# Two-block transformer layer on one Trainium2 core: bias rows of the second expert loop copied into PSUM instead of multiplied in, and one low half in 24 made by GpSimd

## The reference, cut to what matters

```
gu   = t @ w_gu[e] + b_gu[e]          # 2048 columns: 1024 gate, 1024 up
gate = min(gu[:, :1024], 7)
up   = clip(gu[:, 1024:], -7, 7)
h    = (up + 1) * gate * sigmoid(1.702 * gate)
y   += share[e] * (h @ w_dn[e] + b_dn[e])
```

## Time and profile before

| what | value |
|---|---|
| median of three runs | 2695.45 us |
| profiled execution, first to last instruction (its span; the page gives no other time of it) | 2697.9 us |
| busy share of the span: PE, DVE, ACT, POOL | 91%, 80%, 61%, 20% |
| mean granted PE clock | 0.945 of full speed |
| second expert loop | about 1418 to 2668 us of the span |

### The profile page before, as it was taken

One profiled execution on the slowest core, in us unless ns is written; L12 is line 12 of the kernel. 1 busy time (PEld: TensorE's weight loads), 2 busy tenths in 40 slices (PEclk: granted clock), 3 DMA queues, 4 the chain that ended last, 5 costly groups with the idle time before them and its releaser, 6 DMA issues. The chain is left out here.

```text
span 2697.9 us, 38997 instructions
## 1 busy us (share of the span) xinstructions
PE 2455.0 (91%) x11864; PEld 2006.4 (74%) x11864; DVE 2165.1 (80%) x2484; ACT 1639.6 (61%) x1922; POOL 532.6 (20%) x362
## 2 busy tenths in 40 slices
PE   7987858999979998788949999999999999999994
PEld 6846646878768887677737888888888888888883
DVE  7887657999854427886468999999999999999995
ACT  3255536777744326564217777777777777777773
POOL 1213011223200003100021122222222222222220
PEclk9988868999989998999959999999999999999997
DMA  9873236999953410201238999999999999999995
GB/s 347 285 281 107 57 132 246 360 371 383 371 192 111 141 56 1 94 1 63 81 132 310 378 368 364 367 364 366 380 373 366 362 362 362 368 374 377 370 363 169
DMA packets 258910, 711.98 MB, mean 264 GB/s; under 512 B 41377, under 2 KB 74416, under 8 KB 256594
## 3 DMA queue, kind: packets, MB, share of 16 engines
q1 hardware_dynamic: 232626, 640.70, 64.0%
q0 software_dynamic: 22240, 59.81, 7.8%
q10 hardware_dynamic: 3968, 10.49, 1.0%
HBM read 691.95 MB, written 41.49 MB: 272 GB/s over the span
## 5 line engine op out<-in xcount | busy, mean ns | idle before, releaser
L51 PE MATMUL psum_all<-sb_ring_r,sb_arena_r 128*128 128x512 f32 (+1 forms) x2352 | 909.0, 386 | 0.0
L165 DVE TENSOR_TENSOR sb_ring_r<-sb_ring,sb_hi_ring_r 128x1024 fp32r<-128x1024 f32 (+1 forms) x489 | 658.7, 1397 | 124.3 <-ACT sb_hi_ring_r L156 118.5
L156 ACT ACTIVATE sb_arena_r<-sb_ring 128x1024 fp32r<-128x1024 f32 (+1 forms) x462 | 507.5, 1153 | 160.4 <-DMA sb_ring<-in_w_gu_dram 141.6
L165 DVE TENSOR_TENSOR sb_ring_r<-sb_ring,sb_arena_r 128x1024 fp32r<-128x1024 f32 (+1 forms) x462 | 594.0, 1345 | 10.8 <-ACT sb_arena_r L156 10.4
L156 ACT ACTIVATE sb_hi_ring_r<-sb_ring 128x1024 fp32r<-128x1024 f32 (+1 forms) x489 | 554.9, 1193 | 41.9 <-DMA sb_ring<-in_w_in_dram 18.2
L51 PEld LDWEIGHTS psum_all<-sb_ring_r,sb_arena_r 128*128 128x128 f32 x2352 | 447.8, 190 | 93.0
L50 PE MATMUL psum_all<-sb_hi_ring_r,sb_arena_r 128*128 128x512 f32 (+1 forms) x1304 | 497.8, 382 | 15.3 <-DVE sb_ring_r L165 5.2
L52 PE MATMUL psum_all<-sb_hi_ring_r,sb_arena_r 128*128 128x512 f32 (+1 forms) x1304 | 493.7, 379 | 0.0
L50 PE MATMUL psum_all<-sb_arena_r 128*128 128x512 f32 x1064 | 426.8, 401 | 2.5 <-DVE sb_arena_r L2424 2.5
L52 PE MATMUL psum_all<-sb_arena_r 128*128 128x512 f32 x1080 | 427.7, 396 | 0.0
L50 PEld LDWEIGHTS psum_all<-sb_hi_ring_r,sb_arena_r 128*128 128x128 f32 x1304 | 248.4, 190 | 68.5 <-issue 10.2
(11 more groups left out here) (484 smaller groups left out, 3231.8 us busy)
## 6 DMA issues: line engine op xcount, KB each, us to landing
sb_ring<-in_w_gu_dram SPq DMA_DIRECT2D x544, 512.0 KB, 6.3
sb_ring<-in_w_dn_dram SPq DMA_DIRECT2D x272, 512.0 KB, 8.5
sb_ring<-in_w_e_gate_dram SPq DMA_DIRECT2D x36, 1024.0 KB, 7.7
sb_ring<-in_w_e_up_dram SPq DMA_DIRECT2D x36, 1024.0 KB, 7.9
sb_ring<-in_w_e_down_dram SPq DMA_DIRECT2D x36, 1024.0 KB, 7.3
sb_ring<-in_w_in_dram SPq DMA_DIRECT2D x27, 1024.0 KB, 6.5
sb_arena<-in_w_ada_dram POOLq DMA_DIRECT2D x32, 512.0 KB, 5.7
sb_ring<-in_w_mod_dram SPq DMA_DIRECT2D x16, 1024.0 KB, 8.3
```

The source lines that it names most:

```text
L51: eng.matmul(out, a[0], b[1], start=False, stop=False)
L156: act.activation(s.hi[c % len(s.hi)], s.raw[c % len(s.raw)], ACT.Copy).then_inc(s.hi_made, 1)
L165: dve.tensor_tensor(s.lo[c % len(s.lo)], s.raw[c % len(s.raw)], s.hi[c % len(s.hi)].bitcast(F32), ALU.subtract).then_inc(s.lo_made, 1)
```

## The change

The bias matmuls, the selectors and the high and low halves of the bias go. In their place, for each item:

- SP loads the one row of `b_gu` that the item's expert needs (8 KB) into partition 0 or 32 of the tile `rows`, in turns (`bias_row`). Ahead of it SP waits until POOL has widened the first half of the row of the item before (`bias_wide`).
- POOL, after the gather for the next item has landed, spreads that row over all 128 partitions with two `partition_broadcast` of 1024 columns each (`widen`), each once ACT has used the old content of that half (`seeded`).
- ACT copies the wide bias into the two gate banks after the sigmoid of the item before, and into the two up banks after it has read the transposed h (`seed`, two activations of 128 x 1024 from SBUF to PSUM).
- PE's matmuls then only add to what is in the banks, and wait for `seeded`.

Also, the low half of one chunk in 24 (l = 18, the third up chunk) is made by POOL with a tensor_tensor instead of by DVE, and PE waits for it (`pool_lo`). For the first item, `route` ends with one `partition_broadcast` of 2048 columns on POOL, and DVE copies the wide bias into the banks. The core of the diff:

```diff
@@ route @@
-                sp.wait_ge(s.logits, 1)
-                for half in range(2):
-                    sp.dma_start(k.rows[32 * half:32 * half + m.experts].rearrange("p a d -> p (a d)"), b_up
-                                 ).then_inc(R.bias_landed, 16)
             sp.wait_ge(s.items, 1)
             e = sp.value_load(R.expert_i[0:1, 0:1], min_val=0, max_val=E - 1)
+            if biased:
+                sp.wait_ge(s.logits, 1)
+                for i in range(2):
+                    row = e if i == 0 else sp.value_load(R.expert_i[0:1, 1:2], min_val=0, max_val=E - 1)
+                    sp.dma_start(bias_row(k, i), b_up[bass.ds(row, 1)]).then_inc(R.row_landed[i], 16)
...
+            if biased:
+                pool.wait_ge(R.row_landed[0], 16)
+                pool.partition_broadcast(bias_wide(k), bias_row(k, 0))
+def bias_row(k, parity):
+    return k.rows[32 * parity:32 * parity + 1].rearrange("p a d -> p (a d)")
+def bias_wide(k):
+    return k.arena[:, BIAS_AT:BIAS_AT + 2 * D]
@@ experts, sync @@
+                        if biased:
+                            sp.wait_ge(s.bias_wide, 2 * j - 1)
+                            sp.dma_start(bias_row(k, (p + 1) % 2), m.bias[0][bass.ds(expert(j + 1), 1)]
+                                         ).then_inc(R.row_landed[(p + 1) % 2], 16)
@@ experts, gpsimd @@
+            def widen(half, j, parity, count):
+                pool.wait_ge(R.row_landed[parity], 16 * count)
+                pool.wait_ge(s.seeded, 2 * j - 1 + half)
+                pool.sem_inc(s.settled, 1)
+                row = bias_row(k, parity)[:, half * m.width:(half + 1) * m.width]
+                pool.partition_broadcast(seeds[half], row).then_inc(s.bias_wide, 1)
+                pool.wait_ge(s.bias_wide, 2 * j - 1 + half)
...
                         gather(j + 1)
+                        if biased:
+                            pool.wait_ge(s.gathered, 16 * j + 32)
+                            widen(0, j + 1, (p + 1) % 2, i + 2)
+                            widen(1, j + 1, (p + 1) % 2, i + 2)
+                            c = POOL_LO - nB
+                            pool.wait_ge(ss.hi_made, PER * j + c + 1)
+                            pool.tensor_tensor(ss.lo[c % len(ss.lo)], ss.raw[c % len(ss.raw)],
+                                               ss.hi[c % len(ss.hi)].bitcast(F32), ALU.subtract).then_inc(s.pool_lo, 1)
                         scatter(j - 1)
@@ experts, tensor @@
+                    if per and c == POOL_LO - nB:
+                        pe.wait_ge(s.pool_lo, j)
                     if i == 0 and biased:
-                        for b in range(BANKS):
-                            at_col = (BANKS * half + b) * 512
-                            pe.matmul(k.psum[:, UP + BANKS * half + b, :], sel_up[p], bias_hl[:, at_col:at_col + 512],
-                                      start=True, stop=False)
+                        pe.wait_ge(s.seeded, 2 * j + half + 1)
@@ experts, scalar @@
+            def seed(half, j):
+                act.wait_ge(s.bias_wide, 2 * j - 1 + half)
+                act.wait_ge(s.part_read, 2 * j - 1 + half)
+                act.activation(up_banks(half), seeds[half], ACT.Copy).then_inc(s.seeded, 1)
...
                             if l == HT_BEFORE + after(1):
                                 read_h(j - 1)
+                                seed(1, j)
                             if l == nA + after(2):
                                 sigmoid(j)
+                                seed(0, j + 1)
@@ experts, vector @@
-                            make_lo(dve, k, ss, c, PER, j, c in WHOLE)
+                            make_lo(dve, k, ss, c, PER, j, c in WHOLE or l == POOL_LO)
-                            select(sel_up[(p + 1) % 2], j + 1, s.sel_up)
```

More of the change, by code:

```diff
@@ L44, with split3 @@
 SKIP = 4096
+BIAS_AT = 22528
 CONTEXT_BANKS = (4, 5, 6, 0)
[L48 to L52, removed]
+def split3(eng, out, a, b, start, stop, seeded=False):
+    eng.matmul(out, a[0], b[0], start=start, stop=False, skip_group_check=seeded)
+    eng.matmul(out, a[0], b[1], start=False, stop=False, skip_group_check=seeded)
+    return eng.matmul(out, a[1], b[0], start=False, stop=stop, skip_group_check=seeded)
 def chain(eng, sem):
@@ L1795, in route @@
     R.bias_landed = nc.alloc_semaphore(name=f"{name}_bias_landed")
+    R.row_landed = [nc.alloc_semaphore(name=f"{name}_row_landed{i}") for i in range(2)]
     biased = m.bias is not None
@@ L2073, in experts @@
     WHOLE = m.whole
+    POOL_LO = nB + nA + 2 if m.bias is not None else PER
     HT_BEFORE = SPLIT * max(1, nA // SPLIT - 2)
@@ L2094, in experts @@
     if biased:
-        bias_hl = take(m.bias[0].shape[1], True)
-        bias_raw = k.rows[0:64].rearrange("p a d -> p (a d)")
-        sel_up = [take(P, True) for _ in range(2)]
+        seeds = [bias_wide(k)[:, half * m.width:(half + 1) * m.width] for half in range(2)]
         b_down, comb_t = k.pair.rearrange("p a d -> p (a d)"), take(P)
@@ L2101, in experts @@
     more_hi = [take(CHUNK, True) for _ in range(SLOTS - HI_SLOTS)]
-    assert at[0] <= ARENA
+    assert at[0] <= (BIAS_AT if biased else ARENA)
     FIRST = SLOTS * SPLIT
@@ L2200, in _ @@
             if biased:
+                pool.wait_ge(s.gathered, 32)
+                widen(0, 1, 1, 1)
+                widen(1, 1, 1, 1)
                 pool.wait_ge(R.y_ready, 16 * TT)
@@ L2256, in up @@
                             ins = split3(pe, out, (x_hi[p][:, kd, :], x_lo[p][:, kd, :]), [x[:, kk, cols] for x in w],
-                                         kd == 0 and not biased, kd == KD - 1)
+                                         kd == 0 and not biased, kd == KD - 1, biased)
                     ins.then_inc(ss.chunk_used, 1)
@@ L2380, in _ @@
                     sigmoid(0, False)
+                    if biased:
+                        seed(0, 1)
             with act.Fori(0, PAIRS) as i:
@@ L2407, in _ @@
             n = dve.value_load(R.last[0:1, 0:1], min_val=0, max_val=R.max_items - 1) + 1
-            def select(dst, j, sem):
-                dve.tensor_scalar(dst[0:64, :], wide(k.half_row[:, 0], 1, P), R.expert_f[0:64, bass.ds(j, 1)], None,
-                                  ALU.is_equal).then_inc(sem, 1)
             def lo_x(j, p):
@@ L2457, in _ @@
             if biased:
-                dve.memset(bias_hl[64:P, :].bitcast(F32), 0.0)
-                for sel in sel_up:
-                    ins = dve.memset(sel[64:P, :].bitcast(F32), 0.0)
-                ins.then_inc(s.bias_zero, 1)
-                dve.wait_ge(R.bias_landed, 96)
-                dve.tensor_copy(bias_hl[0:64, :], bias_raw).then_inc(s.bias_hi, 1)
-                dve.wait_ge(s.bias_hi, 1)
-                dve.tensor_tensor(bias_hl[32:64, :], bias_raw[32:64, :], bias_hl[32:64, :].bitcast(F32),
-                                  ALU.subtract).then_inc(s.bias_lo, 1)
-                select(sel_up[0], 0, s.sel_up)
-                select(sel_up[1], 1, s.sel_up)
+                for half in range(2):
+                    dve.wait_ge(s.y_made, half + 2)
+                    dve.tensor_copy(up_banks(half), seeds[half]).then_inc(s.seeded, 1)
             make_lo(dve, k, ss, 0)
```

17 lines of the change are left out of this document (7 added, 10 removed).

## The result

The changed kernel takes 2728.75 us (median of 4 runs, 2723.62 to 2745.65) against 2697.14 of the kernel before on the same chip (4 runs, 2695.42 to 2699.04): ratio 1.0127, 95% interval [1.0109, 1.0145]. It is slower by 1.3%, where 2682.6 was forecast. The profiled execution took 2731.62 us, its span is 2729.9.

What follows compares the result with a forecast made beforehand. PE sets the pace at 36.24 us an item, DVE and DMA close behind; afterwards DVE bounds at 33.20 + 2.1 + 0.55 = 35.85, over 33 items 12.9 us faster, so 2682.6 us (forecast's own range 2672 to 2692, whole range 2664 to 2744).

Steps and rivals of the forecast that it cites:

- floor 35.32: PE in the second loop: removing two pairs of bias matmuls saves 0.92 us an item, down to 35.32.
- DVE's exclusion: DVE's low halves wait while POOL reads SBUF: 2.1 us an item for POOL's low half, 0.55 for broadcasts.
- I count half of one broadcast, with its tail, as felt: 0.55: DVE: first broadcast hides beside PSUM work, second partly behind a wait for ACT; cost 0.55 us an item.
- DVE's idle time: DVE in the loop: idle 0.96 and 0.75 us an item before; expected to shrink to nearly none.
- DMA: Transfers in the loop: floor between 34.4 and 36.2 us an item, 35.3 taken, so not the bound.
- ACT's sigmoid seed and SP: Gate-bank seed covered by ACT's 1.28 us idle before the sigmoid; SP's new wait covered by some 7 us.
- Ends: Outside the loop: routing stage and start of the experts, set to 0 in sum, between -2 and +4 us.
- The sum: Item falls from 36.24 to 35.85 us, bound by DVE; over 33 items 12.9 us faster.
- The first rival: Both broadcasts stop DVE, 1.2 us each: 37.7 an item, 2743.6 us, slower; chance 0.27.
- The two signs named for the forecast being wrong: DVE not slowed at all by POOL's low half, or a broadcast taking over 2 us.
- Transfers: Rival: transfers bound the loop, an item stays at 36.1 to 36.24 us, 2691 to 2695 in all; chance 0.13.
- POOL starves: Rival: DVE holds up POOL's low half, PE waits at l = 18, over 2825 us; 0.10 together with longer broadcasts.

Runs made afterwards that it cites:

- e2: Changed kernel without the second loop's two broadcasts an item (items 1 to 33 add item 0's bias row), POOL's low half kept; 2674.3 us.
- e3: Changed kernel without both the loop's broadcasts and POOL's low half, seeds kept; 2677.09 us.
- e6: Changed kernel without POOL's low half, each broadcast of the second loop replaced by a POOL memset of the same tile; 2674.75 us.
- e4: Kernel before with only POOL's low half of l = 18 added, bias matmuls and selector kept; 2695.93 us, ratio 0.9992.
- e1: Changed kernel with DVE making all 24 low halves, none on POOL; broadcasts and seeds kept; 2719.46 us.
- e13: Changed kernel without POOL's low half, with ACT's seed of the up banks behind the high half of l = 11, not 7; 2701.12 us.
- e11: Changed kernel without POOL broadcasts or POOL's low half; each bias half written to all 128 partitions by DMA from DRAM; 2711.9 us.
- e12: Changed kernel with item 0's bias spread by a DMA in the routing stage instead of POOL's broadcast, loop untouched; 2722.73 us.
- e10: Changed kernel without POOL's low half; broadcasts beside DVE's PSUM reads, gather between them, up seed later, item 0's bias by DMA; 2669.33 us.
- e5: Changed kernel without POOL's low half, broadcasts moved beside DVE's PSUM reads, gather queued behind both; 2731.55 us.
- e9: Changed kernel without POOL's low half, broadcasts beside PSUM reads, up seed later, plus an 8-column broadcast starting the routing stage; 2723.82 us.

## Why the prediction was wrong

**PE.** Right: floor 35.32 worked out, 35.27 to 35.30 measured wherever DVE had room (e2, e3, e6).

**DVE's exclusion.** The mechanism was right, and it was priced at 2.1 for POOL's low half (measured 1.76; 1.59 in e2, 1.58 in e4) and 0.55 for the broadcasts. The second is one of the two steps that failed: "I count half of one broadcast, with its tail, as felt: 0.55". Measured are 1.16 in the changed kernel, where by luck some first broadcasts lie beside L2470, and 1.81 to 1.92 with both beside low halves (e1, e13). The 1.2 guessed for one alone was near (1.30). What was wrong was its place. The broadcast was taken to start at the gather's landing, and that to lie where DVE reads PSUM. It starts 6.6 to 9.1 us after the landing, behind the change of kind on POOL, for which the prediction had no term; and the place was checked for the old frame only, though it shifts with the item's length and POOL's other work.

**DVE's idle time.** This is the other step that failed, and the larger. The sum had none left, without a reason given. Measured is 1.00 an item: 10.7 us in the loop for the high half behind the seed of the up banks, 8.2 for PE after POOL's late low half, 6.6 for the reading of h, the rest in short gaps. The prediction covered the seed of the gate banks with the sigmoid. For the one behind L2351 it said only that the low half "must wait for ACT anyhow", and took the wait as a hiding place, not as a cost. e13 gives its price where it occurs in every item: 0.6 an item, 18 us. In the changed kernel, where it occurs in every second one, it is 0.35. The other two parts were not varied by themselves.

**DMA.** Right in kind: not the bound at 13.3 MB an item (376 GB/s in e3, PE never idle). e11 shows how close it is: with 1 MB more an item the transfers bound, at 392 GB/s.

**ACT's sigmoid seed and SP.** Covered, as said: in e3 both stand, and the floor is reached.

**Ends.** Set at 0, between -2 and +4; measured 5.5 late at the loop's start, 7.9 if counted from the first row of the routing stage on POOL (1364.8 in place of 1367.2). The broadcast's duration was right (2.30 within 1.9 to 4.7), but the 8.50 us ahead of it was no row of the trace before. e12 puts its price at some 6 us, on a wide interval.

**The sum.** 35.85 was forecast; 33.20 + 1.16 + 1.76 + 1.00 = 37.1 came. The difference is 0.61 more for the broadcasts, 0.34 less for POOL's low half and 1.00 of idle time. The forecast's gain was 0.39 an item, a difference between sums of 36. Without the idle time the item would have had about its old length (36.12); the idle time turned the sign. The first rival had the right bound (DVE past 36.24), the right sign and nearly the right price (37.7 an item forecast, 37.03 found; "2.4 of broadcasts" was too much, and no idle time was in it); 2728.75 lies inside the range. The first rival's signs came too: slowed low halves beside broadcasts, PE waiting for L166, a pitch over 36.3. The two signs named for the forecast being wrong did not (DVE was slowed by POOL's low half, and a broadcast took 1.87): they looked at durations, and what failed was a place and a wait. *Transfers* did not happen. *POOL starves* did not happen in the changed kernel as it was told, by a low half that can't get in; but its sign, PE waiting for POOL at l = 18, did, 21.5 us in all, because the low half started late. e10's one bad item shows that POOL can starve.

Open is how much of the shift from e1's 2.0 low halves an item beside broadcasts to the changed kernel's 1.29 is due to the 6.6 to 9.1 us and how much to POOL's low half shifting the scatter and so the gather (neither was varied by itself), what POOL does in that time, and what decides whether a broadcast or the low halves go first when both want to run.

Exclusion for the whole instruction, which the prediction took from the Trainium skill (SBUF — State Buffer, Who interferes with whom) as the ground of its rival, is borne out: 0.9 us for a broadcast beside low halves (e1), none beside PSUM readers (e5), none from memsets (e6). That page gives the ports to whoever issues first; in e10's bad item a copy that takes 0.75 otherwise ran for 14.54 us, while DVE started and ended ten low halves, so the turn seems not to go by time of issue alone.

## What to carry to other kernels

Where DVE is the bound and its instructions have two inputs in SBUF, work moved to POOL unloaded DVE here only where POOL's instruction did not read SBUF, or where DVE was just then reading PSUM: 1.14 us moved away cost 1.6 to 1.8, and the same two broadcasts cost low halves 1.8 to 1.9 us or, by place, 0.7 and less (e10, e5). Tie such an instruction to a count of the engine that it must not meet, not to a transfer's landing, and look at once at what is queued behind it. Look in POOL's queue for MODIFY_POOL_CONFIG before letting two kinds of instruction take turns there. And where the forecast gain is a hundredth of a sum, list the idle times of the new bound engine as terms of their own before calling a sign.

## What was not expected of the hardware

- A partition_broadcast of 1 row to 128 x 1024 takes POOL 1.30 us alone and 1.87 on average in the changed kernel's loop; beside low halves it stops them for 0.9 us (e1).
- POOL stood 8.4 to 9.5 us before a partition_broadcast behind tensor_scalars (all kernels that have it in the routing stage), and again on the second one (e9). In the loop it stands so at each change between broadcast and tensor_tensor: 6.6 to 9.1 us past the gather's landing ahead of the broadcast and at least 7.4 ahead of the low half (changed kernel). With broadcasts alone in the loop it is 0.4 (e1).
- POOL's low half, which DVE makes in 1.22, took 2.0 to 3.9 us beside DVE, and DVE lost 1.6 to 1.8.
- Over a whole item, 392 GB/s was the most that the loop moved; 376 to 378 did not slow PE.
